# Attention tiles taken three steps apart in place of two, and the score tail's scratch moved onto the scores' own columns

## What is computed

```python
def chunked_rel_attention(q, k, v, rel_bias):
    ...
    scores = jnp.einsum('bnqhd,bnkhd->bnhqk', qc, kb).astype(jnp.float32) * (dh ** -0.5)
    scores = scores + bias[None, None]
    scores = jnp.where(valid[None, :, None, None, :], scores, jnp.float32(-1e30))
    p = jax.nn.softmax(scores, axis=-1).astype(v.dtype)
    out = jnp.einsum('bnhqk,bnkhd->bnqhd', p, vb)
```

## Time and profile before

| | |
|---|---|
| median of 3 runs | 3867.09 us (3866.86 to 3868.06) |
| the profiled execution's own time | 3866.86 us |
| its span in the profile | 3865.5 us |
| PE busy | 3718.8 us, 96% |
| VectorE, ScalarE, GpSimd busy | 43%, 30%, 28% |
| mean granted PE clock | 0.982 of full |

### The profile page before, as it was taken

The page is one execution under the profiler, slowest core; times in us unless marked ns, Lnnn a source line. Parts: engine busy times, 40 slices in busy tenths (PEclk is TensorE's granted clock), DMA queues, the critical chain, the costliest instruction groups (busy, mean ns, idle before and its releaser), DMA issues.

```text
span 3865.5 us, 41782 instructions
## 1 busy us (share of the span) xinstructions
PE 3718.8 (96%) x17644; PEld 3038.5 (79%) x17644; DVE 1653.6 (43%) x2017; ACT 1149.6 (30%) x1442; POOL 1063.7 (28%) x708
## 2 busy tenths in 40 slices
PE   6999999999999989999999999998999999999998
PEld 6889887888878866777778888887777778888886
DVE  5564525999643244224232222224557652222226
ACT  5554522222231333444121111212332341111123
POOL 3333321222233531102322222222112442222223
PEclk9999999999999989999999999999999999999999
DMA  2000011111232221011211111112111221111112
GB/s 101 28 28 28 28 66 60 55 55 55 71 141 88 98 83 35 33 33 33 87 33 49 49 44 49 44 50 85 33 34 35 102 71 45 49 49 44 49 44 77
DMA packets 60666, 216.68 MB, mean 56 GB/s; under 512 B 6720, under 2 KB 6848, under 8 KB 60352
## 3 DMA queue, kind: packets, MB, share of 16 engines
q1 hardware_dynamic: 60480, 214.01, 16.7%
HBM read 188.82 MB, written 25.17 MB: 55 GB/s over the span
## 4 chain that ended last, share of the span: by engine, by line
PE 87%; DVE 7%; ACT 2%; issue 2%; POOL 1%; DMA 1%; SPq 0%; DVEq 0%; ACTq 0%
PE psum L464 76%; PE psum L576 2%; PE psum L798 2%; PE psum L813 2%; PE psum L828 1%; PE psum L528 1%; PE psum L513 1%; DVE Ab L1950 1%; DVE qb L1996 0%; POOL hl L2841 0%; PE psum L661 0%; DVE k L2538 0%; PE psum L698 0%; DVE hl L1853 0%; PE psum L600 0%
## 5 line engine op out<-in xcount | busy, mean ns | idle before, releaser
L2824 POOL TENSOR_TENSOR wl<-raw,wh 128x512 fp32r<-128x512 f32 x588 | 810.2, 1399 | 2365.7 <-ACT wh L1101 2365.7
L464 PE MATMUL psum<-hh,wh 128*128 128x512 f32 (+2 forms) x3760 | 1163.7, 392 | 63.0 <-POOL wl L2824 13.6
L464 PE MATMUL psum<-hh,wl 128*128 128x512 f32 (+2 forms) x3760 | 1124.4, 382 | 0.0
L464 PE MATMUL psum<-hl,wh 128*128 128x512 f32 (+2 forms) x3760 | 1120.7, 381 | 0.0
L464 PEld LDWEIGHTS psum<-hh,wh 128*128 128x128 f32 x3760 | 676.1, 191 | 212.3 <-issue 38.8
L464 PEld LDWEIGHTS psum<-hh,wl 128*128 128x128 f32 x3760 | 699.6, 190 | 136.6
L464 PEld LDWEIGHTS psum<-hl,wh 128*128 128x128 f32 x3760 | 698.8, 190 | 134.1
L1101 ACT ACTIVATE wh<-raw 128x1024 fp32r<-128x1024 f32 x294 | 309.7, 1053 | 772.4 <-PE psum L464 765.8
L464 PE MATMUL psum<-hdh,wh 128*128 128x512 f32 x1024 | 328.3, 398 | 4.4 <-DVE B L2725 4.4
L2378 DVE TENSOR_TENSOR B<-B,psum 128x1024 f32<-128x1024 f32 x114 | 139.2, 1221 | 444.8 <-PE psum L464 444.8
L464 PE MATMUL psum<-hdh,wl 128*128 128x512 f32 x1024 | 326.0, 395 | 0.0
(11 more groups left out here) (405 smaller groups left out, 3016.2 us busy)
## 6 DMA issues: line engine op xcount, KB each, us to landing
raw<-in_wts SPq DMA_DIRECT2D x294, 512.0 KB, 3.5
keep_x<-B SPq DMA_DIRECT2D x16, 512.0 KB, 3.8
X<-in_xin SPq DMA_DIRECT2D x8, 520.0 KB, 5.2
keep_sz<-tmp SPq DMA_DIRECT2D x8, 512.0 KB, 2.9
av<-keep_gr SPq DMA_DIRECT2D x8, 512.0 KB, 3.2
tmp<-keep_sz SPq DMA_DIRECT2D x8, 512.0 KB, 3.6
av<-keep_gc SPq DMA_DIRECT2D x8, 512.0 KB, 3.8
av<-in_xin SPq DMA_DIRECT2D x8, 512.0 KB, 3.6
```

The lines of the kernel that those rows point to most:

```text
L464: ins = pe.matmul(out, w, x[:, k, c0:c0 + width], start=first and n == 0, stop=final and n == 2)
L2824: gp.tensor_tensor(wl[:, s, a], raw[:, s, a], fp(wh[:, s, a]), SUB).then_inc(*c.lo.tick(i, p))
```

## The change

Every engine's attention function gets a loop of 19 counts in place of 18. The product with v is of tile m = n - 3 in place of n - 2. The `yield` moves to the middle of a loop count: QK(n) and the product with v of n-3 stand ahead of it, the transposes of tile n-2 behind it. So in one turn, between two contraction steps, PE now issues the transposes of n-3, QK(n), and the product with v of n-3. On ScalarE a turn holds the copies of n-2 and the exp of n, on VectorE the normalisation of a head stands behind the `yield`, at m = n - 3. Behind loop counts 6 and 12 there is one more `yield`, and of the two empty ones near the end one is gone, so that a job has 24 segments, as many as three projections have turns. TL moves to columns 0 to 127 of bank 5, where the scores' tail also lies. QK(n) waits for the tail copy of n-3, the tail's transposes wait for the max of tile n (for tiles of 640 keys; from n = 16 on for the max of 15) and for the tail copy before, and VectorE's wait for the tail copy ahead of its max is gone.

```diff
-    S, TL, PT, OUT = psum[:, 4:6, :], psum[:, 5, 128:256], psum[:, 6, :], psum[:, 7, :]
+    S, TL, PT, OUT = psum[:, 4:6, :], psum[:, 5, 0:128], psum[:, 6, :], psum[:, 7, :]
 # TensorE
-            for n in range(18):
+            for n in range(19):
+                m = n - 3
...
-                    if nk > 512 and n >= 2 and keys(n - 2)[0] > 512:
-                        pe.wait_ge(*c.at_act("tail", j, n - 2))
+                    if nk > 512 and n >= 3 and keys(n - 3)[0] > 512:
+                        pe.wait_ge(*c.at_act("tail", j, n - 3))
...
-                if n >= 2:
-                    m = n - 2
+                if m >= 0:
...
-                if 1 <= n < 17:
-                    m = n - 1
...
+                yield
+                if 0 <= n - 2 < 16:
+                    m2 = n - 2
...
+                    pe.wait_ge(*c.at_act("exp", j, m2))
                     if nk > 512:
-                        pe.transpose(TL, p[:, 512:640], ident).then_inc(*c.at_pe.tick("tail", j, m))
+                        if n >= 16:
+                            pe.wait_ge(*c.at_dve("max", j, 15))
+                        elif keys(n)[0] > 512:
+                            pe.wait_ge(*c.at_dve("max", j, n))
+                        if keys(m2 - 1)[0] > 512:
+                            pe.wait_ge(*c.at_act("tail", j, m2 - 1))
+                        pe.transpose(TL, p[:, 512:640], ident).then_inc(*c.at_pe.tick("tail", j, m2))
...
-                yield
-            yield
+                if n in (6, 12):
+                    yield
             yield
             pe.wait_ge(*c.at_dve("tn", j, 1))
 # ScalarE
-            for n in range(18):
-                if 1 <= n < 17:
-                    m = n - 1
+            for n in range(19):
+                m = n - 3
+                yield
+                if 0 <= n - 2 < 16:
+                    m2 = n - 2
...
-                if n in (9, 17):
-                    hd = n // 16
+                if m in (7, 15):
...
-                yield
-            yield
+                if n in (6, 12):
+                    yield
 # VectorE
-            for n in range(18):
-                m = n - 2
+            for n in range(19):
+                m = n - 3
...
-                    if nk > 512 and n and keys(n - 1)[0] > 512:
-                        ve.wait_ge(*c.at_act("tail", j, n - 1))
...
                     ve.tensor_scalar(nm, mx, -1.0, None, MUL).then_inc(*c.at_dve.tick("nm", j, n))
+                yield
                 if m in (7, 15):
...
-                yield
+                if n in (6, 12):
+                    yield
             yield
 # SyncE
-            for n in range(18):
+            for n in range(19):
...
                 yield
+                if n in (6, 12):
+                    yield
             yield
```

More of the change, by code:

```diff
@@ L815, in attention @@
                     ins.then_inc(*c.at_pe.tick("pv", j, m))
-                if 1 <= n < 17:
-                    m = n - 1
-                    nk = min(BAND, 128 * (m % 8 + 1))
-                    p = pp_slot(j, m)
-                    pe.wait_ge(*c.at_act("exp", j, m))
-                    if nk > 512:
-                        pe.transpose(TL, p[:, 512:640], ident).then_inc(*c.at_pe.tick("tail", j, m))
-                    if m:
-                        pe.wait_ge(*c.at_act("pT", j, m - 1))
+                yield
+                if 0 <= n - 2 < 16:
+                    m2 = n - 2
+                    nk = min(BAND, 128 * (m2 % 8 + 1))
+                    p = pp_slot(j, m2)
+                    pe.wait_ge(*c.at_act("exp", j, m2))
+                    if nk > 512:
+                        if n >= 16:
[5 more added lines that the diff above has]
+                        pe.transpose(TL, p[:, 512:640], ident).then_inc(*c.at_pe.tick("tail", j, m2))
+                    if m2:
+                        pe.wait_ge(*c.at_act("pT", j, m2 - 1))
                     elif j:
@@ L828, in attention @@
                         ins = pe.transpose(PT[:, b_ * 128:(b_ + 1) * 128], p[:, b_ * 128:(b_ + 1) * 128], ident)
-                    ins.then_inc(*c.at_pe.tick("pT", j, m))
-                yield
-            yield
+                    ins.then_inc(*c.at_pe.tick("pT", j, m2))
+                if n in (6, 12):
+                    yield
             yield
@@ L1465, in attention @@
             yield
-            for n in range(18):
-                if 1 <= n < 17:
-                    m = n - 1
[L1469 to L1472, removed]
+            for n in range(19):
[3 more added lines that the diff above has]
+                    m2 = n - 2
+                    nk, _ = keys(m2)
+                    q = pt_slot(j, m2)
+                    if m2 >= 2:
+                        se.wait_ge(*c.at_pe("pv", j, m2 - 2))
                     elif j:
-                        se.wait_ge(*c.at_pe("pv", j - 1, 14 + m))
+                        se.wait_ge(*c.at_pe("pv", j - 1, 14 + m2))
                     if nk > 512:
-                        se.wait_ge(*c.at_pe("tail", j, m))
-                        se.activation(q[:, 512:640], TL, COPY).then_inc(*c.at_act.tick("tail", j, m))
-                    se.wait_ge(*c.at_pe("pT", j, m))
+                        se.wait_ge(*c.at_pe("tail", j, m2))
+                        se.activation(q[:, 512:640], TL, COPY).then_inc(*c.at_act.tick("tail", j, m2))
+                    se.wait_ge(*c.at_pe("pT", j, m2))
                     w3 = min(512, nk)
-                    se.activation(q[:, 0:w3], PT[:, 0:w3], COPY).then_inc(*c.at_act.tick("pT", j, m))
+                    se.activation(q[:, 0:w3], PT[:, 0:w3], COPY).then_inc(*c.at_act.tick("pT", j, m2))
                 if n < 16:
@@ L1486, in attention @@
                                   accum_out=rsum[:, n // 8, n % 8:n % 8 + 1]).then_inc(*c.at_act.tick("exp", j, n))
-                if n in (9, 17):
-                    hd = n // 16
-                    se.wait_ge(*c.at_dve("ss", j, hd))
-                    se.activation(ss2[:, :], ss2[:, :], SQRT, scale=1.0 / 64, bias=EPS).then_inc(*c.at_act.tick("ss", j, hd))
-                yield
-            yield
+                if m in (7, 15):
+                    se.wait_ge(*c.at_dve("ss", j, m // 8))
+                    se.activation(ss2[:, :], ss2[:, :], SQRT, scale=1.0 / 64, bias=EPS).then_inc(*c.at_act.tick("ss", j, m // 8))
+                if n in (6, 12):
+                    yield
             yield
```

## The result

The changed kernel takes 3893.61 us (median of 4 runs, 3893.46 to 3896.23), the kernel before 3867.54 us beside it. The ratio is 1.0069, with a 95% interval of 1.0051 to 1.0087: slower by 26 us. The forecast was 3895 us.

What follows compares the result with a forecast made beforehand. PE's instruction stream bounds the attention stage, with 2.7 us of waits. Three jobs at 7.4 us and a last at 6.2 give 28.4; with -2 for passages and +2 for clock, 28 us: 3895 us, range 3881 to 3910.

Steps and rivals of the forecast that it cites:

- (a): Tiles 5, 6, 7: the second head's short QK covers too little of ScalarE's copy; PE stands 0.9 us a job.
- (b): Tiles 13, 14, 15: no QK left between transposes and product with v; 3 x 0.9 = 2.7 us a job.
- (c): Tile 15: QK waits for the tail copy because the tail shares the scores' columns; 0.25 us a job.
- (d): End of head 0 on VectorE: its normalisation delays max(11), so QK(12) stands 1.75 us a job.
- (e): End of a job: output transposes wait for the last normalisation, two contraction steps covering it, not three; 0.8 us.
- (f): End of the first three jobs: value transposes wait for ScalarE's evacuation of v, behind its output copy; 1.0 us each.
- (g): Last job: 1.3 us gained at the max beside the short convolution, 1.1 us lost at the group sums.
- (j): Granted clock: stalls may bring spells at 1.2 GHz; +2 us taken, with 0 and +17 as ends.
- (i): PE's passages from one shape to the next around QK: -2 us taken, bounds -13 and +6.
- rival of hidden copies: Copies are hidden anyway as the passage to QK becomes free: no change that can be told, 3865 us; chance 0.06.
- that of hidden waits: PE's modelled ends hide a wait for VectorE before QK in 24 tiles: faster, 3858 us; chance 0.04.
- that of a normalisation in time: Normalisations are not late, ScalarE's table load being taken up earlier: 3885 us; chance 0.12.
- rival of a falling clock: The clock falls with every cluster of PE stalls in the attention stage: 3908 us; chance 0.14.

Runs made afterwards that it cites:

- drain_apart: The changed kernel with the last three tiles of a job in the old order, a turn between transposes and product with v: 3889.8 us, ratio 1.0060.
- product_first: The changed kernel with the product with v of n-3 ahead of QK(n) in every turn, directly behind its transposes: 3927.2 us, ratio 1.0155.
- order_only: The changed kernel with the tail's transposes back in columns 128 to 255 of bank 5, waits and order kept: 3892.3 us, ratio 1.0066.
- norm_split: The changed kernel with the last two VectorE instructions of head 0's normalisation moved behind max(11): 3886.4 us, ratio 1.0050.
- the mended: The changed kernel with split normalisation, last three tiles in old order, no extra turns behind 6 and 12, and spread convolution: 3871.3 us, ratio 1.0009.
- no_turn_6: The changed kernel without the extra turn behind loop count 6, on all engines: 3892.4 us, ratio 1.0063.
- columns_only: The kernel before, in its own order, with the tail's transposes on columns 0 to 127 and the waits that go with it: 3871.0 us, ratio 1.0008.

## Why the prediction was right

The mechanism was the one forecast, all five waits came where they were put, and the time, 3893.6 against 3895 us, is within 1.4 us. The sum is nearer than its terms, and that nearness is luck. For a job without a slow spell, 7.1 us longer, from starts of PE's instructions and the experiments:

- **(a) short cover.** 0.9 us forecast; 0.35 for tile 5, 0.14 for tile 6, none for tile 7: 0.5. The copy is complete for PE 0.76 us after QK starts, since the passage to QK takes 0.17 us that I had counted as won.
- **(b) bare tiles.** 2.7 forecast, 3.0 measured (4.01 against 3.00 for each turn); drain_apart takes them away and product_first makes more of them.
- **(c) tail.** 0.25 forecast, 0.15 from the starts (0.68 us from the four transposes to QK(15), where it is 0.53 elsewhere). order_only has the same 0.68, so this belongs to the order, and the columns, to which the prediction put it down, cost nothing.
- **(d) normalisation of head 0.** 1.75 forecast, 1.1 measured, shown by norm_split. The chain was right and too long by 0.65: ScalarE's exp(10) started 0.18 us behind its copy and not after it, so its table load began 3.86 us behind the start of PV(7) in place of 4.25, and the contraction step with PT(9) took PE a little longer.
- **(e), (f) end of the job.** 0.8 and 1.0 forecast, 0.8 and 1.05 measured: the two contraction steps with the wait are 3.62 us long where two alone take some 2.85, and the step ahead of the value transposes 2.46 where it takes 1.42.
- **(g) last job.** A gain of 1.3 forecast beside the convolution; it was 2.0: the stall fell from 2.69 to 0.70. The slow clock behind it, 1.5, went with it and is counted in (j). I had taken VectorE's 4.57 us as the price of its instructions, and part of it was GpSimd beside it: 3.51 us in the changed kernel, with a shorter overlap. The loss at the group sums was 0.9 against 1.1.
- **(i) passages.** Forecast -2 us, measured only by what the other terms leave: +0.5 us in a job of the changed kernel, +0.8 in one of the mended, some +2 to +3 us in all. Within its bounds, and of the other sign. A full tile shows it:

```profile
1593.53 0.62 PE L464 MATMUL psum<-hl,wh 128*128 128x512 f32 x2
...
1593.98 0.60 PE L835 MATMUL psum<-cst,pp 128*128 128x128 f32 x4
1594.51 0.29 PEld L799 LDWEIGHTS psum<-ka,qa 64*128 64x128 f32 x2 [0.17 <-issue]
1594.51 1.34 PE L799 MATMUL psum<-ka,qa 64*128 64x512 f32 x4
```

  The idle before QK's weight load fell from 0.36 to 0.17 us, which I had counted, but four transposes now take 0.53 us up to QK, where they took 0.36 up to the projection, and that I had not. The Trainium skill's rule (TensorEngine Tiling (Array Packing), "Key Properties") that a change of tiling mode drains TensorE fits this: QK's weights are 64*128 in the rows and its neighbours' 128*128, and the idle time moved with QK and did not go.
- **(j) clock.** One slow spell in the stage before (1.5 us), one after (1.6): 0 in place of +2. Which late QK(12) brings it is not to be told: it stood 1.03 us in all four jobs, and one of them was followed by 1.2 GHz; with the same wait it was none in order_only, one in no_turn_6 and three in drain_apart. The contraction step at 1780, which the prediction reads as 2.5 us, took 2.70 (1779.92 to 1782.62).

So the terms were off by 0.4, 0.3, 0.1, 0.65 and 1.0 in each job, and by 0.7 and 2 once: (a), (c), (d) and (j) were put too dear, (g)'s gain too small, (b) and (i) too cheap, and most of it cancels. With (i) as the remainder the terms make up the 26.4 us by which the stage is longer (298.52 to 324.91). The total is better than its working. The rival of hidden copies is refuted by the waits of the changed kernel and by product_first, that of hidden waits by columns_only, that of a normalisation in time by norm_split. The rival of a falling clock did not come in the changed kernel but did, in part, in drain_apart and product_first, with five spells each.

## What to carry to other kernels

When a turn's boundary is moved in a hand-ordered pipeline, list for each hand-over what lies between producer and consumer on the waiting engine, and look at the shortest and the last tiles: there the cover is thin or missing, and the steady state shows nothing of it. A greater distance between stages is worth nothing if the boundary then puts a producer, its consumer on another engine, and the answer into one turn. Take a stall from the starts of the instructions around it: here the wait rows named 9.3 us where 13 were lost. And take spells of slow clock out of a stretch before it is compared with an estimate: in product_first they filled the place of a term that the estimate had left out.

## What the hardware showed unexpectedly

VectorE's two `scalar_tensor_tensor` of 128x1024 took 4.57 us in the kernel before, beside GpSimd's two `tensor_tensor` (3.48 us); 3.51 in the changed kernel, where GpSimd's (3.98 us) begin 0.67 us later; and 2.60 in no_turn_6, where nothing overlaps, with GpSimd at 2.53. By these durations some 2 of the 2.7 us of the one stall of the kernel before come from it; this is an estimate, since no run takes the overlap away and leaves the order as it was. The Trainium skill (SBUF — State Buffer, "Who interferes with whom") says that VectorE and GpSimd share one pair of ports under an exclusive lock; by it an engine would be held up in such an overlap, and the traces agree: both engines were slower in it, VectorE by up to 1.97 us and GpSimd by up to 1.45.
